# A four-sub-layer decoder trunk on one core: every P goes through DRAM, and V products move to the steps of other fp32 products

## The reference, cut to what matters

```python
def reference(x, ...):
    for i in range(2):
        g = norm_gains[i]
        h = rmsnorm(x, g[0])
        y = swa_sink_attention(h, ...) if i == 0 else forgetting_attention(h, ...)
        x = x + rmsnorm(y, g[1])
        h = rmsnorm(x, g[2])
        x = x + rmsnorm(swiglu_ffn(h, ...), g[3])
    return x

def swa_sink_attention(h, w_in, sinks, w_out, cos, sin):
    q, k, v = split(h @ w_in); q, k = rotary(q), rotary(k)
    s = mask(q @ k.T * 64 ** -0.5)              # 128 keys back at most
    p = exp(s - m); probs = p / (sum(p) + exp(sink - m))
    return (probs @ v) @ w_out

def forgetting_attention(h, w_in, b_f, w_out):
    q, k, v, f = split(h @ w_in); c = cumsum(log_sigmoid(f + b_f))
    return (softmax(causal(q @ k.T * 64 ** -0.5 + c_t - c_s)) @ v) @ w_out
```

## Time and profile before

| | |
|---|---|
| median of three runs | 2116.84 us |
| the profiled execution, its own time | 2116.7 us |
| its span (first to last instruction) | 2115.0 us |
| PE busy | 2102.2 us, 99% |
| DVE busy | 1604.8 us, 76% |
| ACT busy | 1159.7 us, 55% |
| POOL busy | 146.9 us, 7% |
| granted TensorE clock, mean | 0.999 |
| bytes moved | 418.73 MB, 198 GB/s |

### The profile page before, as it was taken

How to read it: one execution, slowest core, us unless ns; L and a number is a source line. 1 busy time by engine, 2 the same in 40 slices (tenths; PEclk the granted TensorE clock), 3 DMA queues, 4 the chain that set the end, 5 groups by cost and what they waited for, 6 DMA issues and landing times.

```text
span 2115.0 us, 32215 instructions
## 1 busy us (share of the span) xinstructions
PE 2102.2 (99%) x9651; PEld 1720.5 (81%) x9651; DVE 1604.8 (76%) x3283; ACT 1159.7 (55%) x2077; POOL 146.9 (7%) x291
## 2 busy tenths in 40 slices
PE   9999999999999999999999999999999999999998
PEld 7877888888888888888778777888888888888886
DVE  6797677887667777678798888478777678776686
ACT  7766565544455454555665557565444555445553
POOL 2110000000000000000253241000000000000000
PEclk9999999999999999999999999999999999999999
DMA  7797766655666655665687676656565665656662
GB/s 260 213 249 198 198 206 210 193 189 174 197 198 199 198 179 179 198 216 156 192 243 219 209 228 212 200 180 211 188 188 179 198 213 190 187 175 204 211 189 89
DMA packets 217597, 418.73 MB, mean 198 GB/s; under 512 B 15168, under 2 KB 22496, under 8 KB 217008
## 3 DMA queue, kind: packets, MB, share of 16 engines
q1 hardware_dynamic: 211648, 399.30, 60.8%
q0 software_dynamic: 5584, 18.16, 3.1%
q10 hardware_dynamic: 288, 0.33, 0.0%
HBM read 406.16 MB, written 11.57 MB: 198 GB/s over the span
## 4 chain that ended last, share of the span: by engine, by line
PE 50%; DVE 1%; issue 1%; ACT 0%; POOLq 0%; POOL 0%; DVEq 0%
PE bank L1373 16%; PE bank L1374 16%; PE bank L1375 16%; PE bank L1461 1%; PE bank L1422 1%; DVE ring_lo L841 0%; DVE k_t L901 0%; DVE q_t L912 0%; PE bank L1386 0%; PE bank L1433 0%; ACT y_sb L640 0%; PE bank L1405 0%; POOLq L163 0%; POOL post_r L1232 0%; DVE x_sb L1201 0%
## 5 line engine op out<-in xcount | busy, mean ns | idle before, releaser
L1373 PE MATMUL bank<-ring_hi,a_hi 128*128 128x512 f32 x2240 | 882.0, 394 | 1.0 <-DVE ring_lo L841 1.0
L1374 PE MATMUL bank<-ring_lo,a_hi 128*128 128x512 f32 x2240 | 872.5, 389 | 0.0
L1375 PE MATMUL bank<-ring_hi,a_lo 128*128 128x512 f32 x2240 | 872.4, 389 | 0.0
L627 ACT ACTIVATE ring_hi<-stage,g_t 128x512 fp32r<-128x512 f32 x992 | 660.5, 717 | 366.9 <-DMA stage<-ffn_w_gate_up 205.3
L841 DVE SCALAR_TENSOR_TENSOR ring_lo<-stage,g_t,ring_hi 128x512 fp32r<-128x512 f32 x992 | 707.0, 756 | 161.0 <-ACT ring_hi L627 158.8
L1373 PEld LDWEIGHTS bank<-ring_hi,a_hi 128*128 128x128 f32 x2240 | 420.5, 188 | 94.7 <-issue 7.3
L1375 PEld LDWEIGHTS bank<-ring_hi,a_lo 128*128 128x128 f32 x2240 | 420.4, 188 | 89.0
L1374 PEld LDWEIGHTS bank<-ring_lo,a_hi 128*128 128x128 f32 x2240 | 420.7, 188 | 84.2
L839 DVE TENSOR_TENSOR ring_lo<-stage,ring_hi 128x512 fp32r<-128x512 f32 x480 | 305.8, 687 | 136.5 <-ACT ring_hi L625 135.4
L625 ACT ACTIVATE ring_hi<-stage 128x512 fp32r<-128x512 f32 x480 | 277.7, 624 | 178.9 <-PE bank L1375 150.7
L1373 PE MATMUL bank<-ring_hi,h_hi 128*128 128x512 f32 x704 | 274.4, 390 | 0.0
(11 more groups left out here) (156 smaller groups left out, 836.3 us busy)
## 6 DMA issues: line engine op xcount, KB each, us to landing
stage<-ffn_w_gate_up SPq DMA_DIRECT2D x352, 512.0 KB, 4.6
stage<-ffn_w_down SPq DMA_DIRECT2D x176, 512.0 KB, 5.6
stage<-fox_w_in SPq DMA_DIRECT2D x96, 512.0 KB, 4.9
stage<-swa_w_in SPq DMA_DIRECT2D x48, 512.0 KB, 4.6
stage<-swa_w_out SPq DMA_DIRECT2D x64, 256.0 KB, 4.9
stage<-fox_w_out SPq DMA_DIRECT2D x32, 512.0 KB, 4.8
first_scratch<-first_blocks SPq DMA_DIRECT2D x12, 384.0 KB, 5.0
p_f<-first_scratch SPq DMA_DIRECT2D x48, 96.0 KB, 3.8
```

The lines of the kernel that those rows point to most:

```text
L627: nc.scalar.activation(ring_hi[:, n % RING, :], src, ACT.Identity, scale=g_t[:, row * KT + j:row * KT + j + 1]).then_inc(hi_ready, 1)
L1373: nc.tensor.matmul(dst, hi_a, hi_w, start=start, stop=False)
L1374: nc.tensor.matmul(dst, hi_a, lo_w, start=False, stop=False)
L1375: return nc.tensor.matmul(dst, lo_a, hi_w, start=False, stop=stop)
```

## The change

The last group of each layer gets its P through DRAM like the others: `turned`, `transpose_p`, `read_probabilities` and their semaphores are gone, and DVE, SP and POOL turn, store and load P for groups 3 and 7 too. The tables of steps move. In the first layer scores go from steps 6 and 22 to 10 and 28, so that the next group's scores stand at the steps of the V products (42 and 60); loads go from 20 and 24 to 28 and 32. In the second layer the V products, which stood at four steps by one pair, stand at two steps by two pairs. The transposes of the first layer's queries for t = 1 go from step 4 to 7, those for t = 0 from 22 to 28, and POOL does the rotary part ahead of the sinks of pairs 2 and 3. The output projection interleaves three chunks instead of two. Between layer 0's FFN and layer 1 the transposes of x for t = 1 go from steps 9, 12, 14, 18 to 11, 13, 15, 19.

```diff
-STD = dict(scores={6: (0, 1), 22: (2, 3)},
-           maxima={6: (0, 1), 8: (2, 3), 22: (4, 5), 24: (6, 7)},
+STD = dict(scores={10: (0, 1), 28: (2, 3)},
+           maxima={10: (0, 1), 12: (2, 3), 28: (4, 5), 30: (6, 7)},
...
-           scaled={9: 0, 13: 1, 25: 2, 29: 3}, turned={},
+           scaled={13: 0, 17: 1, 31: 2, 35: 3},
+           stored={16: 0, 20: 1, 32: 2, 36: 3}, loaded={28: 0, 32: 1, 44: 2, 48: 3},
            pv={42: (0, 1), 60: (2, 3)}, out={43: 0, 61: 1})
-LAST = dict(scores={6: (0, 1), 24: (2,), 31: (3,)},
...
-            turned={15: 0, 17: 1, 19: 2, 21: 3, 33: 4, 35: 5, 38: 6, 40: 7},
-            pv={32: (0, 1), 43: (2, 3)}, out={})
+LAST = dict(scores={10: (0, 1), 28: (2,), 33: (3,)},
...
+            scaled={14: 0, 18: 1, 31: 2, 37: 3},
+            stored={16: 0, 20: 1, 32: 2, 40: 3}, loaded={28: 0, 32: 1, 44: 2, 48: 3},
+            pv={42: (0, 1), 60: (2, 3)}, out={})
 FOX = dict(scores={14: (0, 1), 34: (2, 3)},
...
-           pv={49: (0,), 60: (1,), 69: (2,), 80: (3,)}, out={61: 0, 81: 1})
-FOX_LAST = dict(scores={14: (0, 1), 34: (2, 3)},
...
-                pv={43: (0, 1), 60: (2, 3)}, out={})
-QK_ATTENDED = 22
+           pv={60: (0, 1), 110: (2, 3)}, out={61: 0, 111: 1})
+FOX_LAST = dict(scores={18: (0, 1), 38: (2,), 50: (3,)},
...
+                pv={64: (0, 1), 86: (2, 3)}, out={})
+QK_ATTENDED = 28
...
-X_STEPS = {1: (8, 11, 14, 18), 2: (9, 12, 14, 18), 3: (8, 11, 14, 18)}
+X_STEPS = {1: (8, 11, 14, 18), 2: (11, 13, 15, 19), 3: (8, 11, 14, 18)}
...
-P_STORED = {12: 0, 16: 1, 28: 2, 32: 3}
-P_LOADED = {20: 0, 24: 1, 40: 2, 44: 3}
...
+OUT_LAST = tuple((c, t, 12, 16) for c in range(3) for t in range(2))
...
+INTERLEAVED = 3
...
-            if s == 4 and (holds_qk(u - 1) and not is_v(u) or u >= U_FOX and is_v(u)):
+            if s == (7 if u < U_FOX else 4) and (holds_qk(u - 1) and not is_v(u) or u >= U_FOX and is_v(u)):
...
-            def read_probabilities(G, i, j):
-
-                act.wait_ge(pt_done, p_number(G, j) + 1)
-                nc.scalar.activation(turned_columns(G)[:, j % 4, :], pt_ps[:, 0:3 * P], ACT.Identity).then_inc(pt_read, 1)
...
                             normalise(G, i, when["scaled"][at_step])
-                            if turned_by_dma(G):
-                                turn_probabilities(G, i, when["scaled"][at_step])
+                            turn_probabilities(G, i, when["scaled"][at_step])
...
             for u in (0, 2, 3, 4, 5, 6):
+                if u < 6:
+                    rope(u, 0)
                 if u >= 3:
                     set_sinks(u - 3, 2)
                     set_sinks(u - 3, 3)
                 if u < 6:
-                    rope(u, 0)
+                    rope(u, 1)
                     if u >= 2:
                         set_sinks(u - 2, 0)
                         set_sinks(u - 2, 1)
-                    rope(u, 1)
...
                         for m in (2, 3):
                             store_probabilities(c, m)
+                        for m in (2, 3):
                             load_probabilities(c, m)
...
-            def transpose_p(G, i, j):
...
-                for k in range(3):
-                    last = nc.tensor.transpose(pt_ps[:, k * P:(k + 1) * P], prob[:, j % 4, k * P + (k > 0):][:, 0:P], ident[:, :])
-                last.then_inc(pt_done, 1)
```

More of the change, by code:

```diff
@@ L296, in weights @@
             n_out, kp = out_chunk(u), pr
-            if n_out is not None and n_out < 2:
-                n_out, j = OUT_TILES[UT * n_out + PAIR * pr]
+            if n_out is not None and n_out < INTERLEAVED:
+                n_out, j = OUT_TILES[u >= U_FOX][UT * n_out + PAIR * pr]
                 kp = j // PAIR
@@ L412, in score_bank @@
             m, a = divmod(h, 2)
[L413 removed]
+            if (G + 1) % NG == 0 and m >= 2:
                 return bank[(5, 7)[a]]
@@ L507, in wait_swept @@
             ffn = ffn_part(u)
-            if t == 1 and out_chunk(u) == 0:
-                eng.wait_ge(tile_used, UT * u + 28)
+            n_out = out_chunk(u)
+            if t == 1 and n_out is not None and n_out < INTERLEAVED:
+                eng.wait_ge(tile_used, UT * (u - n_out) + 40 + 4 * n_out)
             elif t == 1:
@@ L729, in unit @@
                 for s in range(STEPS):
-                    if s == 0 and u > 1 and ffn_part(u - 1) is None and out_chunk(u - 1) != 0:
+                    if s == 0 and u > 1 and ffn_part(u - 1) is None and out_chunk(u - 1) not in range(INTERLEAVED):
                         read_projection(u - 1, i, 1)
@@ L1057, in unit @@
                                 read_transposed(v, i, t)
-                        if u + 1 in (U_SWA_OUT, U_FOX_OUT) and s in EARLY_O:
-                            o_rests(0 if u < U_FOX else 1, *EARLY_O[s])
-                        if n in (0, 1):
+                        if u + 1 == U_SWA_OUT and s in EARLY_O:
+                            o_rests(0, *EARLY_O[s])
+                        if u + 1 == U_FOX_OUT and s in EARLY_O_FOX:
+                            o_rests(1, *EARLY_O_FOX[s])
+                        if n is not None:
                             for kp, t in (LATE_O if u < U_FOX else LATE_O_FOX).get(STEPS * n + s, ()):
@@ L1351, in _ @@
                             bias(c, j)
-                        if c == NG - 1:
-                            for j in range(4, GH):
-                                bias(c, j)
-                            break
                         store_probabilities(c, 0)
@@ L1444, in times_v @@
                     pe.wait_ge(o_read, outputs_read(G, m // 2) + 2 * i)
-                for part, (lo, hi) in enumerate(((0, 2 * P), (2 * P, 3 * P))):
+                for part in range(2):
                     for a in range(2):
-                        if part == 0 and not turned_by_dma(G):
-                            pe.wait_ge(pt_read, p_number(G, 2 * m + a) + 1)
-                        elif part == 0 and a == 0 and G < NG:
+                        if part == 0 and a == 0 and G < NG:
                             pe.wait_ge(first_loaded[m % 2], 64 * (2 * G + m // 2 + 1))
@@ L1463, in times_v @@
                     last.then_inc(pv_done, 1)
-                elif G >= NG and turned_by_dma(G):
-                    last.then_inc(pv_pair, 1)
             def qk_unit(G):
@@ L1507, in input_block @@
                     pe.wait_ge(xt_lo, x_part(b, t, j // 4)[0] + 1)
-                if out_chunk(u) in (0, 1) and j % 2 == 0:
+                if out_chunk(u) in range(INTERLEAVED) and j % 2 == 0:
                     pe.wait_ge(ot_lo[t], 8 * (0 if u < U_FOX else 1) + j // 2 + 1)
```

150 lines of the change are left out of this document (59 added, 91 removed).

## The result

| | before | changed |
|---|---|---|
| median of 20 runs | 2116.67 us | 2120.69 us |
| lowest and highest | 2115.9 to 2117.0 | 2118.5 to 2122.5 |
| profiled execution, its own time | 2116.7 us | 2121.5 us |
| its span | 2115.0 us | 2119.6 us |
| granted TensorE clock, mean | 0.999 | 0.995 |

The ratio is 1.0019, 95% interval 1.0012 to 1.0025: 4.0 us slower (2.5 to 5.3), and still within the 0.2% that was called no change. The forecast was 2109.6, 11.1 us too low, and the time lies above the range, on the other side of the kernel before.

A forecast was written before the change was run, and what follows sets the result against it. The prediction took PE's own program to bound the kernel, not weights, DVE or ACT. From 2116.7 us it took 11.7 off and added 4.5 for the new wait: 2109.5, so 2109.6 as median, range 2105.0 to 2114.5.

The forecast's parts named there:

- The sum on PE: PE's insertions between products: transposes, V products, scores and stalls together 11.7 us off, before the new wait.
- the shared entry: V products right behind scores on PE, 8 places: 0.33 us saved each, 2.6 us off.
- The stalls: PE's transposes of queries (POOL late) and of x (DVE late): waits of 0.64 and 0.96 end, 1.6 us off.
- The wait: First layer, step 42, groups 0 to 3: PE's V products wait for the load of pair 1, 4.5 us in all.
- late by 1.1, 0.7, 1.7 and 1.0 us: 4.5 us: Lateness of pair 1's load against its V product at step 42, for groups 0 to 3.
- The prediction's own sign of being wrong: Step-42 waits for `p_f`, forecast at 0.6 to 1.6 us: absent or twice as long would show the forecast wrong.
- The landing: Pair 1's four loads: the last, issued 1.5 us behind the first, lands 3.8 us later by the median.
- Rival two, the store ahead: The 384 KB store ahead of pair 1's load holds it back: 11.3 us of waits, 2116.4 us; chance 0.15.
- the slower case: PE's wait for pair 1 delays ACT's step-43 read, then DVE and SP's next load: 18 us, 2123.1; chance 0.05.
- Loads in time: Pair 1's loads land before their V products at step 42, no wait: 2105.1 us; chance 0.25.
- The upper bound of 11.3 us for the waits: Waits for pair 1 in groups 0 to 3 if each load lands 1.7 us later: 4.5 + 4 x 1.7.
- DVE's extra work: DVE turns eight more pairs, 1.0 us each, beside PE: costed at nothing, up to 8 us if its lead were gone.

The follow-up runs named there:

- the two edits on SP and ACT: Changed kernel with first-layer loads of pairs 0 and 1 at step 28, queries' transposes at step 30, ACT's read of step 60's V result one step later: 2105.25 us.
- The experiment: Changed kernel with first-layer queries' transposes moved from step 28 to 30 and ACT reading step 60's V result one step later: 2114.73 us.
- early loads: Changed kernel with the loads of pairs 0 and 1 both at step 28 in the first layer, ahead of the store of pair 2: 2109.85 us.
- queries' block back: Against the two edits on SP and ACT: second block of the queries' transposes on DVE at step 20 again, not 22; 2109.20 us.

## Why the prediction was wrong, point by point

**The sum on PE held, from below.** 11.7 us were forecast off without the new wait; with the two edits on SP and ACT 11.4 come, and 2.3 of waits are left, so 13.7 without them. Its terms hold within 0.4 us, but for the shared entry (1.6 and not 2.6), and two gains that it did not have: the forget gate (1.8), and some 0.03 us for each insertion that goes, because the matmuls behind one are a few ns late beyond the second, where the measure stopped (3.2 us behind all insertions of the kernel before, 2.2 with both edits). The stalls came out as forecast in sum, 0.8 and 0.8 for 0.64 and 0.96. But the 0.8 of x stay gained only because the blocks of keys and queries were moved as well: with either put back, PE waits at that block instead.

**The wait was seen, placed and mis-sized**, and that decided the sign. The step that failed is "late by 1.1, 0.7, 1.7 and 1.0 us: 4.5 us". PE stood 3.08, 0.72, 3.92 and 2.90 us, and with the clock the four places cost 18.0. The prediction's own sign of being wrong, waits twice as long, came true in three groups of four. Three things stood in its place:

1. The landing. It was taken at the median of 3.8 us in a stretch where store and weights were queued. Group 0 had 7.4 from the first issue in place of 5.3; with the store behind the load it was 5.7. Rival two, the store ahead, was right as a mechanism in group 0, with its price of 1.7; in groups 2 and 3 the order is worth 0.3 and 0.8 of landing, and in groups 1 and 2 the sum's 5.3 held with the store ahead. The Trainium skill, DMA: Bandwidth & Descriptors, Queues, rings and completion order, says that a DMA's semaphore is raised only after every earlier write of that DMA engine, across its queues. The two orders in group 0 agree with it, 7.4 and 5.7 us; a bandwidth shared with the store would do the same, and no run here tells these two apart.
2. The engine between. The chain went from PE over DVE to SP and had no ACT in it. The change put V products and transposes right behind the scores, and ACT's reads of both stand ahead of the exponentials in ACT's order. "A wait on PE gives DVE the same time to catch up" was the argument against the slower case; in groups 2 and 3 it did not hold, DVE stood for ACT, and SP issued 2.8 and 1.9 us later than in the sum. The experiment shows this cause for group 2; for group 3 the same edit took off 0.5 us of issue, so the rest of its lateness stays open. The prediction's slower rival had the right engine, at another instruction: it looked at the read of step 43 and not at those behind step 28.
3. The clock. No term allowed that a wait costs more than its length. After 3.08, 3.92 and 2.90 us of idleness the products ran at 0.43 us: 3.7 us, and 2.0 more inside the three V products (1.48 us each and not 0.80). The Trainium skill, TensorE: Matmul & The Clock Gate, What's actually happening, says that the throttled clock is the default and that activity releases it; the trace agrees, with 0.50 behind the wait and 1.00 where the wait was filled with matmuls.

**Loads in time** (0.25) would have been 2105.1; with the loads moved the kernel takes 2105.25 and 2104.25. So the forecast of that case was met in the number, but by luck: 2.3 us of waits and 1.0 of shared entry that it did not have stand against 1.8 at the forget gate and 1.1 behind insertions, which it did not have either. Its condition was not met by the change. The upper bound of 11.3 us for the waits was passed because the bound moved the landings alone.

**What was left out** was readable: the list of waits had 1.5 us for `fz` and 0.2 for `z_t` beside the 1.0 that the prediction called the only one for weights. Asking of each wait what stands ahead of its releaser on that engine leads to the queries' block, which the change moves by two steps.

**DVE's extra work** was costed at nothing. With both edits PE waits nowhere for DVE in the first layer; with the early loads alone, where ACT still held DVE up in group 2, it waited 1.6 us.

## What to carry to other kernels

A load that is moved close to its use is priced by the landing with what is queued in that stretch and not by the median of the run, and its chain is followed through every engine that has a read of the same PE step at the head of its queue. A wait of two microseconds or more on PE can cost more than its length, as the matmuls behind it may run at the half clock (0.43 us apart and not 0.227); the kernel with such waits also spread over 4 us in 20 runs, the one with the loads in time over 0.7 in 5. A wait that is taken away gave another engine time to catch up, so the next wait for that engine is looked up too: the 0.8 us at x came back at the gate when a block there stayed where it had been. When the sum on the bound engine is right, a slower kernel can still hold all the gain: here a load moved by four steps, a read of ACT by one and the queries' transposes by two turned 4.0 us more into 11.4 less.

## What the runs showed of the hardware

- The granted clock fell to 0.50 behind idle times of PE of 2.07 us (early loads), 2.90, 3.08 and 3.92 us (changed kernel), and stayed at 1.00 behind 1.74 us (both edits), 2.44 us (exponentials ahead, group 3) and 2.69 us (queries' block back). In the run with PE kept busy in group 0, group 3's wait of 2.45 us was followed by the half clock. So between 2.07 and 2.69 us the length of one wait did not settle it, nor did the DMA traffic: its share was 1.00 in the wait of 2.44 us and 1.03 in that of 2.45 (in that of 2.69 it was 0.00). These two rows, in this order:

```profile
211.38 0.87 PE L1411 MATMUL bank<-p_f,v_sb 128*64 128x256 f32 x8 [2.44 <-DMA p_f<-first_scratch]
```
```profile
213.92 1.55 PE L1411 MATMUL bank<-p_f,v_sb 128*64 128x256 f32 x8 [2.45 <-DMA p_f<-first_scratch]
```

- Scores and V products, both fp32 but of different operands and tile shape, share 0.20 us of entry; two V products share 0.36.
- Four DMAs of 96 KB let PE go on 5.7 us behind the first issue with a 384 KB store behind them, and 7.4 with it ahead, in group 0; in groups 2 and 3 it was 5.0 and 5.3, and 4.9 and 5.7.
- Behind an insertion the 128x512 matmuls start 2 to 7 ns further apart than the 0.227 us, up to about the tenth: 0.03 us for each insertion in the kernel before.
